# Two more seven-product sets in the output projection of a hybrid decoder layer, and one sum moved in VectorE's order

## The reference, cut to what matters

```python
u = rmsnorm(h, g_pre)
p = u @ w_in                      # 4096 x 12296
... four branches (two attentions, S5, RG-LRU), each times SiLU of its gate ...
mixed = jnp.concatenate([o_fox, o_sb, o_ssm, o_lru], axis=-1) @ w_out    # 256 x 4096 times 4096 x 4096
return h + rmsnorm(mixed, g_post)
```

## Time and profile before

| | us |
|---|---|
| three timed executions | 1504.18, 1504.94, 1505.47 (median 1504.94) |
| the profiled execution, its own time | 1504.9 |
| its span in the trace | 1503.2 |
| TensorE busy in it | 1491.6 (99% of the span), granted clock 0.999 |
| VectorE, ScalarE, GpSimd busy | 1066.9, 911.4, 110.8 |

### The profile page before, as it was taken

One profiled execution on the slowest core, in us unless ns is written; L12 is line 12 of the kernel. 1 busy time (PEld: TensorE's weight loads), 2 busy tenths in 40 slices (PEclk: granted clock), 3 DMA queues, 4 the chain that ended last, 5 costly groups with the idle time before them and its releaser, 6 DMA issues.

```text
span 1503.2 us, 21445 instructions
## 1 busy us (share of the span) xinstructions
PE 1491.6 (99%) x6986; PEld 1228.4 (82%) x6986; DVE 1066.9 (71%) x1322; ACT 911.4 (61%) x1233; POOL 110.8 (7%) x161
## 2 busy tenths in 40 slices
PE   8999999999999999999999999999999999999998
PEld 7888888888888888888888888888888888888886
DVE  5665469899888895665564555455547899898987
ACT  6645476666766666666665454466657666565653
POOL 0000011111201110000000101000000000000000
PEclk9999999999999999999999999999999999999999
DMA  8565656565555656565565555555556776667777
GB/s 318 182 196 158 193 165 199 186 197 176 188 184 181 196 172 193 186 192 184 189 219 183 176 167 175 188 171 164 164 185 195 239 244 217 224 223 240 238 245 273
DMA packets 88586, 299.36 MB, mean 199 GB/s; under 512 B 10184, under 2 KB 13520, under 8 KB 88400
## 3 DMA queue, kind: packets, MB, share of 16 engines
q1 hardware_dynamic: 78480, 280.27, 56.9%
q0 software_dynamic: 1872, 6.82, 2.5%
q10 hardware_dynamic: 8176, 11.54, 2.2%
HBM read 294.38 MB, written 4.20 MB: 199 GB/s over the span
## 4 chain that ended last, share of the span: by engine, by line
PE 97%; DMA 1%; DVE 1%; ACT 0%; issue 0%; SPq 0%; ACTq 0%; DVEq 0%
PE main L445 23%; PE main L447 23%; PE main L446 23%; PE main L718 5%; PE main L720 5%; PE main L719 5%; PE side L718 2%; PE side L720 2%; PE side L719 2%; DMA w_raw<-in_wall 1%; PE main L486 1%; PE main L632 1%; PE side L573 1%; PE main L584 1%; PE main L634 1%; PE side L665 0%
## 5 line engine op out<-in xcount | busy, mean ns | idle before, releaser
L1271 DVE TENSOR_TENSOR w_lo<-w_raw,w_hi 128x1024 fp32r<-128x1024 f32 x394 | 483.3, 1231 | 372.1 <-ACT w_hi L839 370.9
L839 ACT ACTIVATE w_hi<-w_raw 128x1024 fp32r<-128x1024 f32 x394 | 413.7, 1057 | 358.4 <-PE main L447 333.7
L445 PE MATMUL main<-w_hi,acts 128*128 128x512 f32 x1532 | 604.9, 395 | 0.5 <-DVE acts L1402 0.5
L447 PE MATMUL main<-w_hi,acts 128*128 128x512 f32 x1532 | 596.9, 390 | 0.0
L446 PE MATMUL main<-w_lo,acts 128*128 128x512 f32 x1532 | 596.4, 389 | 0.0
L445 PEld LDWEIGHTS main<-w_hi,acts 128*128 128x128 f32 x1532 | 287.7, 188 | 62.3 <-issue 3.7
L447 PEld LDWEIGHTS main<-w_hi,acts 128*128 128x128 f32 x1532 | 287.6, 188 | 60.8
L446 PEld LDWEIGHTS main<-w_lo,acts 128*128 128x128 f32 x1532 | 287.9, 188 | 58.4
L857 ACT ACTIVATE w_hi<-scr 128x1024 fp32r<-128x1024 f32 x54 | 57.3, 1060 | 58.3 <-PE side L720 30.1
L718 PE MATMUL main<-w_hi,acts 128*128 128x512 f32 x236 | 91.9, 389 | 0.0
L720 PE MATMUL main<-w_hi,acts 128*128 128x512 f32 x236 | 91.8, 389 | 0.0
(11 more groups left out here) (403 smaller groups left out, 1632.3 us busy)
## 6 DMA issues: line engine op xcount, KB each, us to landing
w_raw<-in_wall SPq DMA_DIRECT2D x455, 512.0 KB, 3.5
scr<-in_wall SPq DMA_DIRECT2D x42, 512.0 KB, 4.5
cross<-in_wall SPq DMA_DIRECT2D x14, 512.0 KB, 6.6
scr<-in_wall POOLq DMA_DIRECT2D x13, 512.0 KB, 7.5
br<-in_x SPq DMA_DIRECT2D x16, 256.0 KB, 7.8
w_raw<-in_wglu SPq DMA_DIRECT2D x8, 512.0 KB, 3.3
out<-br SPq DMA_DIRECT2D x5, 512.0 KB, 2.7
vals<-in_gpost ACTq DMA_DIRECT2D x8, 256.0 KB, 6.4
```

The costliest lines, as they stand in the source:

```text
L445: pe.matmul(main[:, bank0 + a, :], u_h, wh, start=(k == 0), stop=False)
L447: mm = pe.matmul(main[:, bank0 + a, :], u_l, wh, start=False, stop=(k == NK - 1))
L839: act.activation(w_hi[:, c % RING, :], w_raw[:, c % RING, :], ACT.Copy).then_inc(hi_ready, 1)
L1271: dve.tensor_tensor(w_lo[:, c % RING, :], w_raw[:, c % RING, :], w_hi[:, c % RING, :].bitcast(F32), ALU.subtract).then_inc(lo_ready, 1)
```

## The change

1. `GROUPS`: the third pair gets set 3 in the place of the plain `both(3)`, and its order becomes `0, both(1), 2, 3, both(5), 4, 6, lower_first(7)`. The last pair gets set 3 in the place of `both(3)`: `0, both(1), 2, 3, 4, one_column(0, 10)`. So the pairs have 2, 4, 5 and 4 seven-product sets. Two such sets stand next to each other twice in the third pair, and three in the last.
2. Combs of set 3 are made in the second pair, beside its group `both(3)`. Their sums go to `br` rows 20 to 23, and the combs lie over their own source rows, so ACT's first copy waits for all four sums.
3. DVE's order in every seven-product set. Before: low B11, low B22, sum T2, sum T3, low T1, low B21, sum T4, low T3, low T2, low T4. After: low B11, low B22, low T1, sum T2, low B21, sum T3, sum T4, low T3, low T2, low T4.
4. As b12 is now read later, slot 2 may be loaded again only after B21's low part, no longer after T1's.
5. Some seven-product sets now sit in the `w_raw` half, so POOL waits for `raw_in[2]` or `raw_x[2]`, and two semaphores `t1_in` take turns.

```diff
-COMB_SETS = (4, 6, 0, 2)
+COMB_SETS = (4, 6, 0, 2, 3)
+COMB_SCRATCH = (0, 0, 0, 1, 2)
+OVER_SOURCE = 3
+OVER_ROWS = (12, 14, 28, 30)
...
-RAW_LAST = {0: T3, 1: T4, 2: T1, 3: T2}
+RAW_LAST = {0: T3, 1: T4, 2: B21, 3: T2}
...
-          FULL, FULL,
-          (0, both(1), 2, both(3), 4, one_column(0, 10)))
+          FULL,
+          (0, both(1), 2, 3, both(5), 4, 6, lower_first(7)),
+          (0, both(1), 2, 3, 4, one_column(0, 10)))
...
+                     br[:, 20:24, :].rearrange("p j (k n) -> p j k n", k=KC)]
...
-        COMB_AT, COMB_LATE = {4 + LEAD: 0, 7 + LEAD: 1, 10 + LEAD: 2}, OP0[5]
+        COMB_AT = {4 + LEAD: 0, 7 + LEAD: 1, 10 + LEAD: 2, OP0[5]: 3, OP0[GROUP0[1] + 3] + 1: 4}
...
-                if p < 2:
+                if p < N_PAIRS - 1:
                     pe.wait_ge(comb_lo, 4 * COMB_SETS.index(t) + 4)
...
                     if i == T1:
-                        act.wait_ge(t1_in, 16 * (sums + 1))
+                        act.wait_ge(t1_in[sums % 2], 16 * (sums // 2 + 1))
...
-                    act.wait_ge(comb_sum, 4 * n + q + 1)
+                    act.wait_ge(comb_sum, 4 * n + (4 if t == OVER_SOURCE else q + 1))
...
-                if i == B22:
-                    dve.wait_ge(t1_in, 16 * (sums + 1))
-                    dve.wait_ge(lo_ready, OPS0 + m + 1)
+                if i == T1:
+                    dve.wait_ge(t1_in[sums % 2], 16 * (sums // 2 + 1))
+                    dve.wait_ge(lo_ready, OPS0 + m)
                     dve.tensor_tensor(b22, b22, b12, ALU.add).then_inc(t_sum, 1)
+                if i == B21:
                     dve.wait_ge(t_sum, 3 * sums + 1)
                     dve.tensor_tensor(b11, b22, b11, ALU.subtract).then_inc(t_sum, 1)
-                if i == B21:
-                    dve.wait_ge(t_sum, 3 * sums + 1)
                     dve.wait_ge(lo_ready, OPS0 + m + 1)
                     dve.tensor_tensor(b21, b21, b22, ALU.add).then_inc(t_sum, 1)
...
-            for g in SEVENS:
-                pool.wait_ge(raw_x[2], 16 * raw_count(g))
+            for sums, g in enumerate(SEVENS):
+                pool.wait_ge(raw_x[2] if half_of(g) else raw_in[2],
+                             16 * (raw_count(g) if half_of(g) else RAW0 + raw_count(g)))
```

More of the change, by code:

```diff
@@ L191, in hybrid_trunk @@
         comb_sums = [vals[:, 1, 0:1024].rearrange("p (j k n) -> p j k n", j=4, k=KC),
-                     br[:, 28:32, :].rearrange("p j (k n) -> p j k n", k=KC)]
+                     br[:, 28:32, :].rearrange("p j (k n) -> p j k n", k=KC),
+                     br[:, 20:24, :].rearrange("p j (k n) -> p j k n", k=KC)]
         P1_BANK, P3_BANK, P5_BANK, P2_BANK = main[:, 2, :], main[:, 3, :], side[:, 2, :], main[:, 0, :]
@@ L218, in comb @@
         def comb(t, j):
+            if t == OVER_SOURCE:
+                return br_r[:, OVER_ROWS[j]:OVER_ROWS[j] + KC, :]
             n = (COMB_PLACE.index(t) * 4 + j) * KC
@@ L325, in hybrid_trunk @@
         raw_x = [sem(f"raw_x{n}") for n in range(RING)]
-        t_sum, t1_in, p1_out, s_sum, c_sum = (sem(n) for n in ("t_sum", "t1_in", "p1_out", "s_sum", "c_sum"))
+        t_sum, p1_out, s_sum, c_sum = (sem(n) for n in ("t_sum", "p1_out", "s_sum", "c_sum"))
+        t1_in = [sem("t1_in0"), sem("t1_in1")]
         g_in, xl_in = sem("g_in"), [sem("xl_in0"), sem("xl_in1")]
@@ L1140, in comb_high @@
                 for q, j in enumerate((0, 2, 1, 3)):
-                    act.wait_ge(comb_sum, 4 * n + q + 1)
-                    act.activation(comb(t, j)[:, :, 0:P], comb_sums[n // 3][:, j, :, :], ACT.Copy).then_inc(comb_hi, 1)
+                    act.wait_ge(comb_sum, 4 * n + (4 if t == OVER_SOURCE else q + 1))
+                    act.activation(comb(t, j)[:, :, 0:P], comb_sums[COMB_SCRATCH[n]][:, j, :, :], ACT.Copy).then_inc(comb_hi, 1)
             def sb_block(i):
@@ L1220, in _ @@
                     comb_high(COMB_AT[m - 1])
-                if m - 1 == COMB_LATE:
-                    comb_high(3)
                 if p > 0 and m == OP0[GROUP0[p] + 1]:
@@ L1673, in make_combs @@
                 part = lambda k, a: br[:, k:k + KC, a * P:(a + 1) * P]
-                into = lambda j: comb_sums[n // 3][:, j, :, :]
+                into = lambda j: comb_sums[COMB_SCRATCH[n]][:, j, :, :]
                 done = 4 * n
@@ L1692, in comb_low @@
                     dve.wait_ge(comb_hi, 4 * n + q + 1)
-                    dve.tensor_tensor(comb(t, j)[:, :, P:2 * P], comb_sums[n // 3][:, j, :, :],
+                    dve.tensor_tensor(comb(t, j)[:, :, P:2 * P], comb_sums[COMB_SCRATCH[n]][:, j, :, :],
                                       comb(t, j)[:, :, 0:P].bitcast(F32), ALU.subtract).then_inc(comb_lo, 1)
@@ L1839, in _ @@
                     comb_low(COMB_AT[m - 2])
[L1840 to L1843, removed]
                 if p > 0 and m == OP0[GROUP0[p] + 3] + 1:
@@ L2016, in _ @@
                 fetch_values(h)
-            for g in SEVENS:
-                pool.wait_ge(raw_x[2], 16 * raw_count(g))
+            for sums, g in enumerate(SEVENS):
+                pool.wait_ge(raw_x[2] if half_of(g) else raw_in[2],
+                             16 * (raw_count(g) if half_of(g) else RAW0 + raw_count(g)))
                 c = 2 * KIND[g]
                 pool.dma_start(raw_at(g, 2), wall[B_OUT + 2 * PAIR_OF[g], :, c * CW:(c + 1) * CW],
-                               accum_op=ALU.add).then_inc(t1_in, 16)
+                               accum_op=ALU.add).then_inc(t1_in[sums % 2], 16)
 def _lay_out(v):
```

## The result

The changed kernel takes 1507.37 us (median of 20 runs, 1506.11 to 1508.49) against 1505.13 for the kernel before in 20 runs on the same chips (1504.15 to 1505.86). The ratio is 1.0014, 95% interval 1.0008 to 1.0021: a small loss of 2.2 us, inside the 0.2% that the forecast called no change, and 1.5 us over the forecast of 0.7 more than the profiled execution of before. The range of the forecast was 1502.9 to 1508.4. The rows of the changed kernel come from its longest execution, 1508.49 us, 1.1 over its median; those of the kernel before from one near its median (1504.9).

A forecast was written before the change was run, and what follows sets the result against it. PE was taken to bound the kernel, with DVE the next engine to count. 1504.9 - 2.72 (fewer matmuls) + 1.05 (second sets) + 1.95 (third set) + 0.4 (border) = 1505.6 us; range 1502.9 to 1508.4.

The forecast's parts named there:

- The saving: Two exchanged sets in the projection each save PE six matmuls of 0.2267 us, 2.72 us at most.
- The single sets, the order, the combs: Sets after a plain group, their new DVE order, and set 3's combs in the second pair cost PE nothing.
- The second sets: Sets 3 and 6 of the third pair, set 3 of the last: PE 0.35 late at T3, 1.05 us together.
- The restart: After a wait for DVE's low part, PE's matmul starts 0.17 us after DVE's end.
- the second case of the forecast: After PE's wait the weight load follows in full, 0.03 + 0.22; the sum would be 0.3 us more.
- the first case: TensorE pulls weight loads ahead of matmuls in flight, so starting after a wait costs at most 0.15 us.
- The third set: Set 4 of the last pair: DVE's ten instructions exceed PE's seven ops, so PE waits 1.95 us at T3.
- The border: Before the last pair: lead of 0.4 used up at T2, PE waits 0.4 us at T4 of set 0.
- its likeliest case: Whole kernel: small net loss with PE waiting 2.7 to 5 us; chance 0.66.
- Lead enough: Second and third sets start with more than 2.87 us lead, PE hardly waits: 1502.2 to 1504; chance 0.20.
- Transfers bunch up: Last group's loads meet the eight `g_post` loads at set 4; over 3.0 us slower, up to 1513.8; chance 0.08.
- Waits cost DVE more: DVE instructions with waits queue 1.26 us apart, not 1.14: 4.4 us more, 1510.0; chance 0.06.

The follow-up runs named there:

- the run with 13 sets: The changed kernel with the group lists of before, keeping the new DVE order, late slot 2 and combs of set 3: 1505.09 us, ratio 1.0000.
- the late `weigh`s: The changed kernel with two of DVE's four products with g_post moved from the last group behind low parts of the tail: 1506.41 us, ratio 1.0013.

## Why the prediction was right, and where it was not

**The saving.** 12 matmuls fewer, at 0.227 us, and lost in full to waits: right.

**The single sets, the order, the combs.** No wait in the first two pairs and none in the run with 13 sets: right. The reason given for the combs, a plain group with 6.3 us of free DVE time, doesn't hold for every plain group: put into the plain group behind the border's set 0, they made the second pair lose 3.6 us where the third, with the same sets and no combs, loses 0.8. "After a set it would be all of 3.4" was near that 2.8.

**The second sets.** 0.35 each was forecast, 0.50, 0.35 and 0.50 measured, 1.35 for 1.05. The working is met to 0.02 at set 6. The 0.3 over are two instructions of 128x2 which the forecast did not list in DVE's queue, though the moved set now had them inside; the run without them has 0.35 at all three.

**The restart.** Forecast as 0.17 from DVE's end. Of T3 in set 4, DVE's low part ends at 1454.42 + 1.23 = 1455.65, the matmul starts 0.05 later, and the one behind it 0.11 later than in a free run: 0.16. The trace shows the first weight load at the matmul's own start, 1455.70, not 0.22 ahead of it. The rule weighed in the forecast ("TensorE: Matmul & The Clock Gate" of the Trainium skill, "Step-by-step: what each phase is for") has loads pulled ahead. Here the load was not pulled ahead of the wait, as in the second case of the forecast, and still the sum is not that case's 0.25 but 0.16, close to the 0.15 of the first. So the size is the first case's and the order of events the second's; neither case as put holds.

**The third set.** 1.95 forecast, 1.86 to 1.90 measured. From T3 to T3 DVE takes 11.43 us (1442.99 to 1454.42) without idle time; forecast 11.47. What the forecast did not say is that ten instructions and the trip through ACT bind alike: with nine and the old trip the loss is the same.

**The border.** 0.4 forecast, 0.30 measured, and at T4 as forecast.

**The tail.** This is the step that failed: "the third set ... PE waits 1.95 us" was taken as the end of it. DVE leaves the third set with no lead, and nothing was worked out for what comes behind. There the one plain group has four low parts and four `weigh`s, 9.1 us of DVE against 10.88 of PE, and the tail begins with a low part and the shared sums, 3.9 more. DVE's low parts come 2.0 us later against PE than before, the loads of the slots follow, x loads go beside them, and PE loses 1.74 us. Together with the 0.3 of the second sets, less 0.2 at the third set and the border, this is the forecast's 3.4 turned to 5.25, just over the 5 at which its likeliest case ended. That is of the longest execution; with the 0.69 to 1.25 that five other kernels lose in the tail it would be 4.2 to 4.8. So the time fell into the range because the range was wide, not because the sum had this term.

**The rivals.** *Lead enough*: no, the lead was 2.7 to 2.9 us as read. *Transfers bunch up*: not where it was put (the last group's chunks were in time beside the `g_post` loads), but the mechanism came one stage later, with x loads, at 1.7 us. *Waits cost DVE more*: no; low parts that wait for ACT stand 1.14 apart (1454.26, 1455.40 in the run without sum T4).

**What stays open.** The losses of the sets and the tail give 5.25 - 2.72 = 2.5 us, where 2.2 was measured by the medians; but that trace is of the longest execution. With the late `weigh`s the losses leave 0.8 where 1.6 was measured, and with the order alone 0 where 0.3 was. Of the 0.8 that are missing with the late `weigh`s 0.4 is the last store, which is slower with 15 sets for a reason that no run looked for. The wait at the start of the kernel (L453) differs from one profile to the next, 0.2 to 1.4 us (0.5 before the change), and is large enough for the rest. Whether it differs by kernel or only by run was not tried.

## What to carry to other kernels

When the second engine needs more time for a unit of work than the bottleneck has, count the lead in front of it, take off for each such unit in a row what it lacks, and go on counting behind the last one until the lead is back: the debt is handed to whatever comes next. Here a unit alone was free, a second one in a row cost a third of its gain, a third cost more than its whole gain, and the stage behind paid again. Before an instruction is taken from a queue to make it shorter, look whether the next one would only wait for another engine in its place.

## What the runs showed of the hardware

- A subtraction on DVE with both inputs in SBUF that starts beside an addition on GpSimd stands until GpSimd's is done: it ends 1.08 to 1.09 us after it in all 15 cases, and takes 2.95 to 3.42 us for 128x1024 where the median over the run is 1.22. GpSimd needs 2.4 to 3.3 us for the same size. The Trainium skill's "SBUF — State Buffer", "Who interferes with whom", says that a VectorE instruction with two SBUF inputs contends with a GpSimd instruction that reads SBUF, and that whoever issues first holds the shared pair of ports for its whole instruction while the other is fully blocked. The run agrees: GpSimd started first in all 15 cases.
- A matmul that waited for DVE's low part of T3 starts 0.05 us after that engine's end with its weight load beside it (1455.65, 1455.70 in the changed kernel), and the next one comes 0.34 behind it in place of 0.227; at T4 of the border these were 0.15 and 0.31. The list of waits shows 0.28 less than is lost at such a place, and shows nothing where 0.3 is lost: small waits are found only in the distances of the starts.
